# Raw-token transposes ahead of the router, and a gather of expert 0's tokens that comes out transposed

## What is computed

```python
def rmsnorm(x, g):
    xf = x.astype(jnp.float32)
    y = xf * lax.rsqrt(jnp.mean(xf * xf, axis=-1, keepdims=True) + EPS)
    return (y * g.astype(jnp.float32)).astype(x.dtype)
...
    logits = (xt @ w_router).astype(jnp.float32) + b_router.astype(jnp.float32)
    top_val, top_idx = lax.top_k(logits, TOP_K)
    gates = jax.nn.softmax(top_val, axis=-1)
...
        g = xblk @ w_gate[e] + b_gate[e]
        u = xblk @ w_up[e] + b_up[e]
        g = jnp.minimum(g, SWIGLU_LIMIT)
        u = jnp.clip(u, -SWIGLU_LIMIT, SWIGLU_LIMIT)
        a = (u + 1.0) * (g * jax.nn.sigmoid(SWIGLU_ALPHA * g))
        return a @ w_down[e] + b_down[e]
...
    x = x + moe_ffn(rmsnorm(x, g_ffn), w_router, b_router, w_gate, b_gate, w_up, b_up, w_down, b_down)
```

## Time and profile before

| | us |
|---|---|
| median of 3 runs | 1268.56 |
| lowest and highest of the 3 | 1264.09, 1269.29 |
| the profiled execution, its own time | 1267.07 |
| its span, first to last instruction | 1265.2 |
| TensorE busy | 1205.9 (95%) |
| VectorE busy | 496.5 (39%) |
| ScalarE busy | 191.7 (15%) |
| moved by DMA | 461.29 MB, mean 365 GB/s |

### The profile page before, as it was taken

How to read it: one execution, slowest core, us unless ns; L and a number is a source line. 1 busy time by engine, 2 the same in 40 slices (tenths; PEclk the granted TensorE clock), 3 DMA queues, 4 the chain that set the end, 5 groups by cost and what they waited for, 6 DMA issues and landing times.

```text
span 1265.2 us, 15322 instructions
## 1 busy us (share of the span) xinstructions
PE 1205.9 (95%) x5750; PEld 492.2 (39%) x5750; DVE 496.5 (39%) x1190; ACT 191.7 (15%) x400; POOL 8.1 (1%) x12
## 2 busy tenths in 40 slices
PE   6999989899999999999998999999999999999995
PEld 3665664455333333333332333333333333333331
DVE  2299882344522333422332323233234333332324
ACT  3204442134110101010110001100010000101012
POOL 0000000000000000000000000000000000000000
PEclk9999999899999999999999999999999999999998
DMA  9925377819699999999999999999999999999994
GB/s 341 331 82 155 103 275 270 332 41 368 267 416 423 427 426 426 426 428 426 427 428 426 426 428 428 426 426 427 426 386 386 425 426 428 425 426 428 425 426 172
DMA packets 53251, 461.29 MB, mean 365 GB/s; under 512 B 6217, under 2 KB 15881, under 8 KB 27527
## 3 DMA queue, kind: packets, MB, share of 16 engines
q1 hardware_dynamic: 50831, 448.71, 85.9%
q0 software_dynamic: 1152, 8.39, 1.8%
q10 hardware_dynamic: 1216, 3.47, 0.8%
HBM read 457.64 MB, written 3.28 MB: 364 GB/s over the span
## 4 chain that ended last, share of the span: by engine, by line
PE 75%; DMA 21%; issue 2%; DVE 2%; ACT 0%; POOL 0%; SPq 0%; POOLq 0%; DVEq 0%; ACTq 0%
PE psum L849 39%; DMA ring<-in_w_up 16%; PE psum L831 5%; PE psum L335 5%; PE psum L895 4%; PE psum L389 3%; DMA ring<-in_w_gate 3%; PE psum L599 2%; PE psum L709 2%; PE psum L879 1%; PE psum L373 1%; DMA ring<-in_w_mk 1%; PE psum L715 1%; PE psum L397 1%; PE psum L526 1%
## 5 line engine op out<-in xcount | busy, mean ns | idle before, releaser
L849 PE MATMUL psum<-ring,work 128*64 128x512 f32 x3072 | 676.7, 595 | 22.5 <-DMA ring<-in_w_up 20.4
L849 PEld LDWEIGHTS psum<-ring,work 128*64 128x64 f32 x3072 | 216.3, 137 | 471.2 <-issue 415.9
L831 PE MATMUL psum<-H,work 128*64 128x512 f32 (+1 forms) x384 | 92.7, 600 | 0.0
L2125 DVE TENSOR_TENSOR work<-psum,keep 128x512 f32<-128x512 f32 x16 | 11.1, 691 | 166.0 <-PE psum L849 166.0
L2111 DVE TENSOR_TENSOR X<-X,psum 128x512 f32<-128x512 f32 x68 | 46.6, 685 | 67.2 <-PE psum L895 67.1
L1706 DVE SCALAR_TENSOR_TENSOR ring<-ring,vecT 128x256 f32<-128x256 f32 x240 | 72.6, 377 | 0.1
L2125 DVE TENSOR_TENSOR work<-psum,work 128x512 f32<-128x512 f32 x16 | 11.1, 691 | 141.7 <-PE psum L849 141.6
L1566 ACT COPY work<-psum 64x512 f32<-64x512 f32 x32 | 18.5, 578 | 298.8 <-PE psum L849 298.8
L1554 ACT COPY work<-psum 128x512 f32<-128x512 f32 x31 | 18.2, 586 | 279.2 <-PE psum L831 279.2
L895 PE MATMUL psum<-work 128*128 128x512 f32 x100 | 54.6, 628 | 0.9 <-ACT work L1566 0.8
L335 PEld LDWEIGHTS psum<-C,work 128*128 128x128 f32 (+1 forms) x332 | 44.2, 192 | 25.9 <-issue 20.9
(11 more groups left out here) (313 smaller groups left out, 963.0 us busy)
## 6 DMA issues: line engine op xcount, KB each, us to landing
ring<-in_w_up SPq DMA_DIRECT2D x64, 2048.0 KB, 26.4
ring<-in_w_gate SPq DMA_DIRECT2D x64, 2048.0 KB, 24.2
ring<-in_w_down SPq DMA_DIRECT2D x64, 2048.0 KB, 29.0
ring<-in_cache_keys SPq DMA_DIRECT2D x64, 144.0 KB, 2.7
ring<-in_w_in SPq DMA_DIRECT2D x1, 4096.0 KB, 33.4
ring<-in_mem_keys_turned SPq DMA_DIRECT2D x8, 512.0 KB, 14.3
ring<-in_cache_mem_v SPq DMA_DIRECT2D x8, 512.0 KB, 7.3
ring<-in_w_in SPq DMA_DIRECT2D x1, 2688.0 KB, 24.3
```

What stands on the lines that cost most here:

```text
L831: last = mm(psum[64 * nh:64 * nh + 64, 2, :], Ph[0:ROWS[tt], tt, :], xn[0:ROWS[tt], tt, 512 * nh:512 * nh + 512], start=tt == 0, stop=tt == 2)
L849: last = mm(psum[64 * nh:64 * nh + 64, bank, :], src[:, j, 64 * half:64 * half + 64], w[:, half, j, 512 * nh:512 * nh + 512], start=first ...
L2125: v.tensor_tensor(gm, psum[:, 0, :], B[b][:, 0:512], ALU.add).then_inc(s.g_sum, 1)
```

## The change

The router's transposes now read `X`, the residual stream, and not `xn`: `flip_raw` takes the place of `flip_tile` for the three tiles and waits for the residual add of the tile instead of its normalisation. What is transposed and gained is then x g and not x g / rms, and the reciprocal of the root, which is one number per token, is multiplied in with the bias when the logits are read: three instructions of 32 columns (one for each tile) instead of one of 96. VectorE takes tile 2's transposes before it normalises that tile; the two memsets of the routing table move ahead. `xn` is still made, for the gathers. For expert 0, `gather`, ScalarE's copy and `turn` are replaced by 24 matmuls which have 128 strided columns of `xn` as stationary operand and the 64 columns of `Ph` as moving one, so that the result is already transposed; ScalarE only raises the semaphores for them.

```diff
-            def by_stride(tt, k):
-                return xn[0:ROWS[tt], tt, 512 * (k // 4) + k % 4:512 * (k // 4) + 512:4]
+            def flip_raw(tt):
+                r = ROWS[tt]
+                for kk in range(2 if r == 128 else 1):
+                    n = 4 if r == 128 else 8
+                    ps = V.open(pe, ("h3T", tt, kk))
+                    emptied(pe, V, ("mo", tt, kk if r == 128 else 1))
+                    for k in range(n * kk, n * kk + n):
+                        c0 = 512 * (k // 4)
+                        last = flip(ps[:, r * (k % n):r * (k % n) + r], X[0:r, tt, c0 + k % 4:c0 + 512:4], r)
+                    last.then_inc(s.full_v, 1)
...
-            flip_tile("h3T", 2, 0, by_stride)
+            flip_raw(0)
...
+            pe.wait_ge(s.x_norm, 9)
             pe.wait_ge(s.p_built, 1)
-            gather(s.xg_full)
-            pe.wait_ge(s.xg_moved, 1)
-            turn(3, XG, s.xt_full)
+            for h in range(2):
+                for j in range(4):
+                    for tt in range(3):
+                        last = mm(psum[:, 3, 128 * j + 64 * h:128 * j + 64 * h + 64],
+                                  xn[0:ROWS[tt], tt, 512 * h + j:512 * h + 512:4], Ph[0:ROWS[tt], tt, :],
+                                  start=tt == 0, stop=tt == 2)
+            last.then_inc(s.xt_full, 1)
...
-            act.wait_ge(s.xg_full, 1)
-            nc.scalar.copy(XG, psum[:, 2, :]).then_inc(s.xg_moved, 1)
+            act.wait_ge(s.xt_full, 1)
+            act.sem_inc(s.xg_full, 1)
+            act.sem_inc(s.xg_moved, 1)
...
             norm(2, 1)
+            st(v.memset(routing[:, :, 0:2, :], 0.0))
+            st(v.memset(routing[:, :, 2, :], -1.0))
             add_tile(V, s.free_v, "mo", 2)
             take_tile("h3T", gf[:, :], 1)
+            take_tile("h3T", gf[:, :], 2)
             norm(2, 2)
-            take_tile("h3T", gf[:, :], 2)
-
-
-            st(v.memset(routing[:, :, 0:2, :], 0.0))
-            st(v.memset(routing[:, :, 2, :], -1.0))
...
-            st(v.tensor_tensor(lg, v3(psum[:, 7, 256:352], 32), brb.unsqueeze(1).to_broadcast([P, 3, NE]), ALU.add))
+            for tt in range(3):
+                st(v.scalar_tensor_tensor(lg[:, tt, :], psum[:, 7, 256 + 32 * tt:288 + 32 * tt], small[:, 14 + tt:15 + tt], brb,
+                                          ALU.mult, ALU.add))
```

More of the change, by code:

```diff
@@ L786, in _ @@
                         last.then_inc(s.full_v, 1)
-            flip_tile("h3T", 2, 1, by_stride)
+            flip_raw(1)
             def router_part(c0, c1):
@@ L798, in _ @@
             router_part(0, SEQ)
-            flip_tile("h3T", 2, 2, by_stride)
+            flip_raw(2)
             emptied(pe, V, ("h3T", 2, 0))
```

## The result

The changed kernel takes 1281.92 us (median of 4 runs, 1279.24 to 1283.33) against 1268.92 (1264.09 to 1270.56) before: the ratio is 1.0102, with a 95% interval of 1.0085 to 1.012. It is 13 us, about 1%, slower. The forecast of 1269.6 was wrong, and so was its range, which ended at 1274.

The account below looks back on a forecast made before the run. The end was taken as expert 0's first half product's end plus a weight stream without slack. The profiled 1267.07 us plus 1.7 (gather) and 0.8 (clock), with 0 for the transposes and VectorE's order, gave 1269.6 us; range 1265 to 1274.

Parts of the forecast that it names:

- Where the time is decided: End of expert 0's first half product starts the weight reloads; any shift there moves the kernel's end by as much.
- Part 1: Router transposes read X instead of xn: removes waits for normalisations, gains 0 to 0.1 us, taken as 0.
- Part 2: VectorE's new order and three logits instructions ahead of routing: hidden, taken as 0, bounds 0 and 0.4 us.
- Part 3: Expert 0's new gather: 48 records take 6.1 us against 4.3 for gather, copy and turn, +1.7 us.
- The stride: Strided columns loaded in expert 0's new gather: 0.010 us added to 0.113 per record, taken from transposes.
- the strided load pays in full: Rival, 10%: new gather's records every 0.169 us, 8.2 us in all, +3.9; with the clock 1271.8 us.
- Part 4: TensorE's clock falls around or behind the new gather, slowing the first product: +0.8 us, bounds 0 and 1.6.
- The rival on the other side: Rival, 6%: new gather bound by half clock takes 9.7 us, +5.4, first product loses 1.6: 1274.1 us.

Follow-up runs that it names:

- the repaired gather: Experiment 7's kernel with xn written so that expert 0's transposed gather loads contiguous columns, 128 rows in tile 2: 1268.3 us, ratio 1.0 to the kernel before.
- the flips alone: The change with expert 0's old gather, copy and turn put back; transposes of X and VectorE's new order stay: ratio 0.9997 to the kernel before.
- Experiment 7: The change with the old gather put back and tile 2's transposes moved ahead of the first router part: 1266.18 us, ratio 0.9986 to the kernel before.
- experiment 4: The change with contiguous columns and 128 rows in tile 2 in the new gather: gather 5.54 us, launch 1266.85 us.
- experiment 5: The change with every second column instead of every fourth in the new gather: gather 11.02 us, launch 1276.27 us.
- experiment 8: Experiment 7's kernel with 2 instead of 5 idle matmuls behind the ranks: ratio 1.0003 to the kernel before.

## Why the prediction was wrong

**Where the time is decided: right.** "The end is that product's end plus a stream without slack." From first reload to the span's end it is 941.1 us before, 940.9 after, and 939.1 to 941.0 in all experiments but the repaired gather, over first reloads from 322.8 to 337.7. The 2.6 us of the slow product passed through as well. The repaired kernel's 936.9 is the exception: it regained some 4 us behind its reload, and no run shows by what.

**Part 1, transposes of X for nothing: right.** Shown by the flips alone (0.9997) and by the same distance. The reason given, that tile 2's normalised rows were there when TensorE came to them, fits this. Experiment 7 moves the work itself, and there the distance fell by 0.8.

**Part 2: right.** The three logits instructions take 0.57 where one took 0.26, 0.3 more, under L811; the rest is hidden.

**Part 3, the gather: this step failed.** I put "one every 0.113 us" and "I add that 0.010" for the stride, 6.1 us in all. It took 14.1. The count and the 0.113 for contiguous loads at full clock were right (experiment 4: 0.112). The start was given as within 0.3 us of 315.0 and was 317.37, of which 1.5 arose before the attention's last transposes and 0.9 in the router stage. Two terms were wrong, and a third, the clock's hold on narrow loads, stands under part 4:

- *The stride.* Not 0.010, but 0.234 - 0.112 = 0.122 a record at full clock, 47 x 0.122 = 5.7 us. In the change itself the clock was at half for most of the gather, and taking the stride away saved 14.09 - 10.99 = 3.1. I took the price from transposes, which show as one record each, and carried it over to float32 matmuls, which show as two. The transposes of X read the same step of 16 bytes at 0.12. A price for a float32 matmul's operand, here the moving one, stood in the trace of the kernel before, in expert 20's second pass, whose weights are read in strided order for gate and up and contiguously for down (TensorE's timeline):

```profile
909.19 14.84 PE L879 MATMUL psum<-ring,kvg 128*32 128x256 f32 x128
...
938.29 3.66 PE L879 MATMUL psum<-ring,kvg 128*32 128x256 f32 x64
```

  Per record that is 0.116 against 0.057, a factor of 2.0, both at full clock. Of the bounds, the case "the strided load pays in full" took the factor 1.5 from load lengths; it should have been 2. The rule cited for it, that of the Trainium skill ("SBUF — State Buffer", section "Door 1: The DMA port swizzle"), is that an access to a new 16-byte line pays. The float32 loads agree with it: at full clock a step of four costs 0.234 us against 0.112, a step of two 0.118 (experiment 5). I had let the wrong row overrule it.

- *The 64-row tile.* I wrote nothing of it, so it stood at nothing. It costs 2.7 us. Before, `gather` had it as well, four records of twelve; the new one changes rows 15 times instead of once.

**Part 4, the clock: right in kind, too small.** I had "the clock to fall around or behind it" and took 0.8 of at most 1.6 for the product. It took 2.6, since nearly the whole product ran at half and I had priced one ordinary fallen stretch over a longer stretch of work. That narrow matmuls lose little by the clock was wrong for contiguous loads: 5.54 us at full, 10.34 at half. No row stood behind it, as L511 had run at full clock. For the strided ones, by chance, it held. No one of the three terms explains the miss alone: with the stride out the launch took 1277.43 us, with the 64-row tile out 1276.82, both past 1274; with both out, and the clock at full, it took 1266.85.

The rival on the other side put a gather of 9.7 us and 1274.1 on half clock. Its end was the nearest, its mechanism was not that of the change: there the records did not follow the clock, but the stride. It is the mechanism of the repaired kernel, whose contiguous records took 10.34 us at half clock, and its reason against itself ("these move 64, so half as long") was wrong: they came every 0.213 us, like L811's with 128 columns moving. Sum with the measured terms: 1267.07 + 9.8 (gather) + 2.6 (product) = 1279.5, against 1281.63 for the profiled execution; the 2.2 left are 1.5 ahead of the place, 0.9 in the router stage and -0.2 behind.

## What to carry to other kernels

Price an access pattern by a row of the same kind of instruction: at full clock a float32 operand at a step of 16 bytes went at half rate as stationary and as moving operand, and the one-record transposes next to them, of the same bytes, hid it. Turning few wide matmuls into many narrow ones to save a copy and a turn trades a fixed 1.4 us for loads in single file, which are the longer way even when contiguous (5.5 us against 4.3), and in five of seven profiles the clock fell under them, and the product behind ran at half for the most part. An operand that is ready earlier is worth something only once the work is moved to use it: the raw tokens in their old place gave nothing (0.9997), the reordering 0.1% in experiment 7 and nothing that shows in experiment 8.

## What the runs showed of the hardware that I had not expected

- At full clock a step of two float32 elements cost next to nothing (0.118 against 0.112 us a record), a step of four doubled the spacing (0.234). At half clock contiguous loads came every 0.213 us and those at a step of four still every 0.233.
- Between records of 128 and of 64 rows, TensorE lost time: 0.28 us a group of three tiles at full clock and 0.38 at half, with strided and with contiguous loads; 2.7 us over the 15 changes here.
- While 48 narrow records ran, the clock fell in all five profiles with strided columns or with a 64-row tile; in the two profiles with neither it stayed at full once (5.54 us) and was already at half once (10.34). What decides between these two is open. The old gather was met by a low stretch as well, in experiments 7 and 8 (3.42 and 4.06 us for 2.94).
- The spread between executions of one kernel goes with the granted clock: the kernel before took 1263.6 to 1264.9 us in executions with a mean of 0.993, and 1269.9 to 1272.0 in those with 0.986.
